# Constant products on TensorE ahead of the first weights, the first projection's products in another order, and three short steps of the scan moved later

## What is computed

```python
def even_mixer(xn, positions, w_in, w_out, ...):      # xn = rms_norm(x)
    z = xn @ w_in                                     # [256,1024] @ [1024,2048]
    q, k, v, u = ...                                  # four slices of 512 columns of z
    q = partial_rope(q, positions) * HEAD_DIM ** -0.5
    k = partial_rope(k, positions)
    att = dilated_attention(q, k, v)
    ssm = s5_mixer(u, a_re, a_im, log_dt, ...)        # a linear scan over the 256 rows
    return concatenate([att, ssm]) @ w_out

def s5_mixer(u, ...):
    bu = einsum('gpc,bsgc->bsgp', b_bar, u)           # complex
    h = associative_scan(_linear_combine, (a_bar, bu))
    y = einsum('gcp,bsgp->bsgc', c_mat, h).real + d_skip * u
    ...
```

## Time and profile before

| | us |
|---|---|
| median of 3 timed runs | 1250.57 |
| lowest and highest of them | 1250.17, 1251.11 |
| the profiled execution, first to last instruction (span) | 1248.4 |

### The profile page before, as it was taken

The page is one execution under the profiler, slowest core; times in us unless marked ns, Lnnn a source line. Parts: engine busy times, 40 slices in busy tenths (PEclk is TensorE's granted clock), DMA queues, the critical chain, the costliest instruction groups (busy, mean ns, idle before and its releaser), DMA issues.

```text
span 1248.4 us, 15780 instructions
## 1 busy us (share of the span) xinstructions
PE 1236.7 (99%) x6366; PEld 1031.4 (83%) x6366; DVE 811.4 (65%) x1037; ACT 668.3 (54%) x965; POOL 89.2 (7%) x121
## 2 busy tenths in 40 slices
PE   7999999999999999999999999999999999999998
PEld 6778888888888888888888888888888888888887
DVE  7995756654788766554687746656547785655553
ACT  7865653433898654443687535444436644544431
POOL 2410000000100100000232000000001300000000
PEclk9999999999999999999999999999999999999999
DMA  7344555555554565555554235555555315555551
GB/s 306 105 140 144 190 198 172 199 173 199 189 200 163 192 222 183 192 179 200 181 199 169 68 102 169 202 192 179 184 192 181 131 39 202 199 186 185 183 188 67
DMA packets 32536, 216.60 MB, mean 173 GB/s; under 512 B 3904, under 2 KB 4544, under 8 KB 7376
## 3 DMA queue, kind: packets, MB, share of 16 engines
q1 hardware_dynamic: 30384, 210.32, 48.8%
q0 software_dynamic: 1360, 4.78, 1.2%
q10 hardware_dynamic: 720, 0.50, 0.1%
HBM read 214.54 MB, written 1.05 MB: 173 GB/s over the span
## 4 chain that ended last, share of the span: by engine, by line
PE 93%; DVE 4%; issue 1%; DMA 1%; ACT 0%; SPq 0%; DVEq 0%; ACTq 0%
PE PS L461 26%; PE PS L463 26%; PE PS L462 26%; PE PS L467 6%; PE PS L791 2%; PE PS L815 1%; PE PS L496 1%; PE PS L498 1%; PE PS L495 1%; PE PS L544 1%; PE PS L538 1%; PE PS L539 1%; DVE WL L1748 1%; DMA X<-in_x 1%; DVE YG L2037 1%
## 5 line engine op out<-in xcount | busy, mean ns | idle before, releaser
L1748 DVE TENSOR_TENSOR WL<-RAW,WH 128x2048 fp32r<-128x2048 f32 (+2 forms) x200 | 442.9, 2218 | 310.6 <-ACT WH L1130 310.6
L1130 ACT ACTIVATE WH<-RAW 128x2048 fp32r<-128x2048 f32 (+2 forms) x200 | 371.2, 1858 | 366.4 <-PE PS L463 366.1
L461 PE MATMUL PS<-WH,HTh 128*128 128x512 f32 (+1 forms) x848 | 334.6, 395 | 0.2
L463 PE MATMUL PS<-WH,HTl 128*128 128x512 f32 (+1 forms) x848 | 329.0, 388 | 0.0
L462 PE MATMUL PS<-WL,HTh 128*128 128x512 f32 (+1 forms) x848 | 328.3, 387 | 0.0
L463 PEld LDWEIGHTS PS<-WH,HTl 128*128 128x128 f32 x848 | 159.2, 188 | 33.2
L461 PEld LDWEIGHTS PS<-WH,HTh 128*128 128x128 f32 x848 | 159.4, 188 | 32.0 <-DVE WL L1748 0.8
L462 PEld LDWEIGHTS PS<-WL,HTh 128*128 128x128 f32 x848 | 159.5, 188 | 30.6
L461 PE MATMUL PS<-WH,YAh 128*128 128x512 f32 x402 | 158.6, 394 | 0.1
L463 PE MATMUL PS<-WH,YAl 128*128 128x512 f32 x402 | 156.7, 390 | 0.0
L462 PE MATMUL PS<-WL,YAh 128*128 128x512 f32 x402 | 156.5, 389 | 0.0
(11 more groups left out here) (354 smaller groups left out, 1442.9 us busy)
## 6 DMA issues: line engine op xcount, KB each, us to landing
RAW<-in_w SPq DMA_DIRECT2D x196, 1024.0 KB, 4.9
BC<-in_rows POOLq DMA_DIRECT2D x4, 512.0 KB, 4.0
YG<-in_mem POOLq DMA_DIRECT2D x4, 512.0 KB, 4.7
X<-in_x SPq DMA_DIRECT2D x2, 512.0 KB, 5.4
RAW<-in_w SPq DMA_DIRECT2D x4, 256.0 KB, 6.0
BC<-in_s SPq DMA_DIRECT2D x1, 512.0 KB, 11.6
YG<-in_s SPq DMA_DIRECT2D x1, 512.0 KB, 11.9
BB<-in_s SPq DMA_DIRECT2D x1, 512.0 KB, 12.5
```

The source lines that it names most:

```text
L461: e.matmul(out, ah, bh, start=start, stop=False)
L463: return e.matmul(out, al, bh, start=False, stop=stop)
L1130: e.activation(WH[:, c % NW, w], RAW[:, c % NR, w], ACT.Copy).then_inc(S.hi, 1)
L1748: e.tensor_tensor(WL[:, c % NW, w], RAW[:, c % NR, w], WH[:, c % NW, w].bitcast(f32), SUB).then_inc(S.lo, 1)
```

## The change

1. DVE sets two rows of the tile `YBh` (used only much later) to 1.0 as its first instruction and counts a new semaphore `warm`.
2. PE multiplies this tile with itself, nine times ahead of the first transposes and five times behind them (`idle_products`). The results go to a PSUM bank that is overwritten later and are never read.
3. `first_edge` is rewritten: the same 48 products, in another order. The products with `WL` are taken as late as they may be, and the second half of x is transposed in one go behind the first eight products.
4. In `ev_q`, `u_turn` moves from behind step 2 to behind step 3, `b_turn` from behind step 2 to behind step 4, and `b_first` from behind step 3 to behind step 6.

```diff
+            def idle_products(n):
+                for _ in range(n):
+                    e.matmul(PS[:, 7, :], YBh[:, 0, 0:128], YBh[:, 0:2, :].rearrange("p a b -> p (a b)"), start=True, stop=True)
...
             def first_edge():
...
+                for k in range(4):
+                    e.wait_ge(S.hi, k + 1)
+                    hi(0, k)
+                    rest(0, k)
+                e.wait_ge(S.c_x1, 16)
+                turn(0, 1)
+                for k in range(4):
+                    e.wait_ge(S.lo, k + 1)
+                    lo(0, k)
+                for k in range(4):
+                    hi(1, k)
+                    lo(1, k)
                 for k in range(4):
-                    tk = edge_product(0, 0, PS[:, 1, :], 1, k, slice(512 * k, 512 * k + 512))
+                    tk = rest(1, k)
                 tk.then_inc(S.used, 1)
...
+            e.wait_ge(S.warm, 1)
+            idle_products(9)
             e.wait_ge(S.c_id, 16)
             e.wait_ge(S.c_x0, 16)
             turn(0, 0)
+            idle_products(5)
             first_edge()
...
-            rows_mm(PLAN["ev_q"], 4, 8, 512, HT, (2, 3), at={2: [u_turn, b_turn], 3: [b_first]})
+            rows_mm(PLAN["ev_q"], 4, 8, 512, HT, (2, 3), at={3: [u_turn], 4: [b_turn], 6: [b_first]})
...
             pd = Tally()
+            e.memset(YBh[:, 0:2, :].bitcast(f32), 1.0).then_inc(S.warm, 1)
             e.wait_ge(S.pa, PA["DT"])
```

More of the change, by code:

```diff
@@ L225 @@
     c_c c_id c_x0 c_x1 c_p c_i c_t c_B c_C c_m c_S c_bc c_tb c_gr c_mem c_o0 c_o1
-    fills half fin turn hthi htlo x yg sq var rs hi2 rowsq hsq
+    warm fills half fin turn hthi htlo x yg sq var rs hi2 rowsq hsq
     rsx th sg an fold yhi ylo
@@ L514, in first_edge, with hi @@
-                for i in range(4):
-                    e.wait_ge(S.lo, i + 1)
-                    e.matmul(PS[:, 0, :], HTh[:, i, 0:128], WL[:, 0, 512 * i:512 * i + 512], start=False, stop=False)
-                for k in range(4):
-                    tk = edge_product(0, 0, PS[:, 1, :], 1, k, slice(512 * k, 512 * k + 512))
-                tk.then_inc(S.used, 1)
[L520 to L526, removed]
+                def hi(t, k):
+                    ts, w = slice(128 * t, 128 * t + 128), slice(512 * (k % 4), 512 * (k % 4) + 512)
+                    e.wait_ge(S.hthi, htlo_n(0, t, k))
+                    e.matmul(PS[:, t, :], HTh[:, k, ts], WH[:, k // 4, w], start=k == 0, stop=False)
@@ new lines, in lo, with rest @@
+                def lo(t, k):
+                    ts, w = slice(128 * t, 128 * t + 128), slice(512 * (k % 4), 512 * (k % 4) + 512)
+                    return e.matmul(PS[:, t, :], HTh[:, k, ts], WL[:, k // 4, w], start=False, stop=t == 0 and k == 7)
+                def rest(t, k):
+                    ts, w = slice(128 * t, 128 * t + 128), slice(512 * (k % 4), 512 * (k % 4) + 512)
+                    e.wait_ge(S.htlo, htlo_n(0, t, k))
+                    return e.matmul(PS[:, t, :], HTl[:, k, ts], WH[:, k // 4, w], start=False, stop=t == 1 and k == 7)
@@ new lines, in first_edge @@
+                e.wait_ge(S.hi1, 1)
+                for k in range(4, 8):
+                    if k == 6:
+                        e.wait_ge(S.hi, 5)
+                    hi(0, k)
+                    rest(0, k)
+                for k in range(4, 8):
+                    if k == 4:
+                        e.wait_ge(S.lo1, 1)
+                    elif k == 6:
+                        e.wait_ge(S.lo, 5)
+                    lo(0, k)
+                for k in range(4, 8):
+                    hi(1, k)
+                    lo(1, k)
```

## The result

The changed kernel takes 1256.24 us (median of 6 runs, 1254.01 to 1258.54), the kernel before 1250.37 us beside it (6 runs, 1249.60 to 1251.25). The ratio is 1.0045, with a 95% interval of 1.0035 to 1.0056: slower, by more than the 0.2% that can be told from no change. The direction was forecast; the time, 1253.1 us, was 3.1 us short, and the range ended at 1254.8 us, too low. The six executions lie apart: two, at a mean granted clock of 0.999, took 1254.0 and 1254.4 us, three at 0.996 and 0.997 took 1256.1 to 1256.6 us (the profiled one is among these), and one at 0.994 took 1258.5 us.

The account below looks back on a forecast made before the run. PE, busy for 99% of the span, was taken to bound the kernel. PE's 2.8 us of lateness less 0.3 us of an absorbed wait gave 2.5 us: span 1248.4 to 1250.9 us, median 1253.1 us, range 1250.2 to 1254.8 us.

Parts of the forecast that it names:

- The idle products and the order: Start of the kernel: clock up by 10.62 us, ev_q begins at 21.2 instead of 24.34 us, a lead of 3.1 us.
- Rival A: Start of the kernel: the clock doesn't come up in time, ACT's and DVE's lists start 1.6 us later; 1254.7 us, chance 0.06.
- the bound of 0.3 us: Start of the chain: transposes late by at most 0.3 us; 0.1 us taken for ACT and DVE, bounds 0 and 0.3.
- The first gate: Ahead of step 4 of ev_q: PE waits 2.7 us for chunk 3's remainder and begins step 4 at 30.2 us.
- The lead: Into ev_q: PE 3.1 us ahead, most of it swallowed at the wait for chunk 3's remainder.
- The moved steps: In ev_q: b_first begins at 35.35 us and L2020 at 37.8 us, 3.7 us later than before.
- what DVE regains: DVE behind b_first: operations no longer lengthened beside POOL's L2522 give back 1.4 us, bounds 0 and 1.4 us.
- the second wait: Before ev_k: PE waits 3.2 us for chunk 4's remainder until 42.4 us and goes on 2.8 us later than before.
- the sum: From 42 us to the end: 2.8 - 0.3 = 2.5 us late, span 1250.9 us, median 1253.1 us, bounds 1252.6 to 1254.6 us.
- rival B: In PE's two new waits: the clock falls, 16 to 30 slow products cost another 3 to 6 us; 1256 to 1259 us, chance 0.08.

Follow-up runs that it names:

- e7: The kernel before with only the new order of the first products, no idle products, the scan's steps in their old places: 1250.24 us, ratio 1.0000.
- e3: The changed kernel with 9 never-read products in PE's wait for chunk 3 and 12 in its wait for chunk 4: 1252.75 us, ratio 1.0021.
- e3b: The changed kernel with 12 never-read products in the wait for chunk 4 only, the wait for chunk 3 left idle: 1254.42 us, ratio 1.0032.
- e2: The kernel before with only the scan's three steps moved: 1254.15 us, ratio 1.0030.
- e10: The kernel before with only the three steps moved, and 12 never-read products in PE's wait for chunk 4: 1252.42 us, ratio 1.0017.
- e1: The changed kernel with the scan's three steps back in their old places: 1250.20 us, ratio 1.0000 against the kernel before.
- e8: e1 with POOL's six operations that make CFe cut to 2 of 32 columns, part of the output left out: 1248.28 us, ratio 0.9985.
- e6: The changed kernel with b_first behind step 5 instead of step 6 of ev_q: 1252.80 us, ratio 1.0015 against the kernel before.
- e4: The changed kernel without the memset and the 14 idle products, new order and moved steps kept: 1256.10 us, ratio 1.0048 against the kernel before.

## Why the prediction was wrong, point by point

- **The idle products and the order: right in size, but the cause was only in part the idle products.** The nine products run from 1.44 to about 5.4 us, `ev_q` begins at 21.47 us for 21.2 forecast. Rival A (the clock late) is out. The first transposes start 0.45 us later than before (5.44 for 4.99 us), more than the bound of 0.3 us, and the remainder of chunk 3 starts 0.16 us later (28.04 for 27.88 us), within it. The forecast let the early clock come from the idle products; by e7 the new order alone brings 2.3 of the 2.9 us.
- **The first gate: right.** The lead ends in a wait for the remainder of chunk 3: 2.41 us long, over at 30.39 us (forecast 2.7 and 30.2 us).
- **The moved steps and what DVE regains: right in mechanism and size, once the clock is held.** In e3 the first of the two operations behind `b_first` (L2020, there L2054) starts at 37.51 us (forecast 37.8) and the second wait is over at 42.12 us (forecast 42.4), both 0.3 us early, since in this execution the remainder of chunk 3 starts 0.4 us earlier than before (27.45 for 27.88 us); L2057 and L2552 are short again, as foreseen, and the time is 1252.75 us, inside the forecast's own 1252.6 to 1254.6 us. The lateness at the end of the scan's products is that of the whole run: the last L2021 starts at 74.3 us before and at 76.5 us in e3, 2.2 us later, and the spans differ by 1250.6 - 1248.4 = 2.2 us. The rows (line, count: ns min/median/max, first to last start us), of before and of e3:

```profile
L2021 DVE TENSOR_TENSOR JK<-PS,SX x4: 1214/1215/1215, 35.3 to 74.3; 128x1024 f32<-128x1024 f32 x4
```

```profile
L2055 DVE TENSOR_TENSOR JK<-PS,SX x4: 1215/1216/1219, 38.7 to 76.5; 128x1024 f32<-128x1024 f32 x4
```

- **The step that failed: the sum had no term for the clock.** I saw both waits coming, with nearly their true lengths, named the fall behind them as rival B, priced it at 3 to 6 us, and gave it 0.08, since no row of before showed a fall behind a wait. That was no evidence against it: before has no wait of that length behind which the pace was high, so its trace could not show one either way. With B's lower price, 3 us, the sum is 1256.1 us, and 1256.24 us was measured. The range, cut off at 1254.8 us, left out the case that came. The step says that a new wait costs PE its own length; the runs showed that each of the two also slowed the work behind it, and that this was worth 3.5 us (1256.24 against 1252.75 us with the waits filled). That B's lower price fits so well is in part luck: B counted 16 to 30 slow products, and in after there are twelve, with eight transposes and some short products at the same clock. The Trainium skill ("TensorE: Matmul & The Clock Gate", section "HAM oscillation — how this bites in real kernels") was the one voice for B, as it says that idle stretches between bursts bring the low clock back; the traces of after agree (0.66 and 0.76 behind waits of 2.41 and 3.07 us), and I should have weighed it higher.
- **How the fall adds up.** The first fall lies ahead of `b_first`, which therefore starts at 37.12 instead of the forecast 35.35 us, L2050 at 39.59 instead of 37.8 us, and the second wait ends at 44.19 instead of 42.4 us: 1.8 us later all along. Of this 0.2 us were there at the end of the first wait (30.39 for 30.2 us), so that the fall itself costs 1.6 us by the forecast's sum, and 1.5 us against e3: from the end of the first wait to that of the second it is 13.8 us in after and 12.3 us in e3. By the medians one fall costs 1.7 us (e3b against e3, e2 against e10) and the other 1.8 us. The account, 1250.2 us and 2.6, 1.7 and 1.8 us, gives the measured time back because it is made of differences between these medians; the check on it is that the traces and the second pair agree to 0.2 us.
- **What e1 missed.** I expected about 1.5 us of gain with the steps back. There the swallower isn't chunk 3's gate but, for the most part, POOL: the contention that the forecast counted as going away (1.4 us regained) doubles to 2.8 us, as more of the operations meet. The Trainium skill ("SBUF — State Buffer", section "Who interferes with whom") has the rule, that a DVE instruction with two SBUF inputs contends with GpSimd's reads; e8 agrees with 2.99 against 1.29 us.

## What to carry to other kernels

A wait that a change puts on a TensorE that was running without gaps can have two prices, the time by which it makes the engine late and the slower products behind it; in this kernel the second was larger (3.5 us against 2.6 us). Before moving work out of PE's way, look at what it releases on other engines: here a step of PE that came over 3 us later (L2054 in e3: 37.51 for 34.12 us) held a remainder that PE itself needed next. And an early start is worth only what the next gate lets through: look for the gate that doesn't follow PE, and for the engine that will now run beside another.

## What the runs showed of the hardware

- In the profiled executions the granted clock fell to half behind waits of 2.38 us (e6), 2.41 and 3.07 us (after), and 3.07 us (e2, and e4, there 0.9 us after the work had gone on), and stayed up behind 1.71 us (e6) and 1.88 us (the first wait of e4). After a fall it was back after 3.4 us of work almost without a gap in after; in e4 it took 10.3 us in all, with `b_u(1)`, 32 short products, in that stretch. Why it took three times as long there is open.
- It also fell without a long wait. In the profiled executions of e7 and e8 PE's longest wait near there is 0.5 and 0.6 us, ahead of `b_first`, and yet the products behind `b_first` run at half speed; the stretch of e8:

```profile
30.00:35.00 5.00, 4.94 (x38) 4.00 (x35) 3.98 (x5) 4.97 (x9) 1.40 (x6) 0.73 0.63 211
```

  What lies ahead of that fall is a busy PE with 32 short products in it; e1, with the same products and a wait of 0.6 us, shows 1.00 in its profiled execution. In e8 the runs at a mean clock of 1.000 took 1247.5 to 1248.3 us, those at 0.998 and 0.999 took 1249.3 to 1249.8 us; in e7 the two kinds don't differ (1250.1 to 1250.5 us). The kernel before shows such a spread as well: beside e1, six of its 22 executions had a mean clock of 0.999, and all but one of the other 16 were faster than all six. What decides it from run to run is open, and so is what the clock goes by: that the waits bring their falls is shown by filling them, not why. Eight transposes stand directly ahead of the waits of 2.38 and 2.41 us, and also of the 1.88 us without a fall; whether they have a part in it no run here separates.
- In after the faster pace was there at 6.73 us, behind nine products and eight transposes that followed each other without a gap from 1.44 us on, and it held until the first wait. In e7 it was there by 13.88 us, behind eight products and eight transposes without a gap from 8.34 us on.
